# Stick-breaking heads of a Trainium2 kernel: two heads' value products side by side, clamps in two parts, one projection group moved

## What is computed

```python
def stick_breaking_attention(q, k, v):     # 6 heads, 512 tokens, 64 channels
    z = einsum(q, k)                                        # scores
    log_fail = where(valid, log_sigmoid(-z), 0.0)           # valid: key strictly before query
    after = cumsum(log_fail, reverse=True) - log_fail       # over the keys behind
    wts = where(valid, exp(log_sigmoid(z) + after), 0.0)
    return einsum(wts, v)
...
mixed = concatenate([o_dilated, o_differential, o_stick]) ; return mixed @ w_out
```

## Time and profile before

| | us |
|---|---|
| median of 3 runs | 3336.99 (3336.99 to 3346.36) |
| the profiled execution | 3350.7 |
| its span | 3348.8 |
| PE busy in the span | 3169.2 (95%) |
| DVE busy | 1861.8 (56%) |
| ACT busy | 1261.1 (38%) |

### The profile page before, as it was taken

The page is one execution under the profiler, slowest core; times in us unless marked ns, Lnnn a source line. Parts: engine busy times, 40 slices in busy tenths (PEclk is TensorE's granted clock), DMA queues, the critical chain, the costliest instruction groups (busy, mean ns, idle before and its releaser), DMA issues.

```text
span 3348.8 us, 60877 instructions
## 1 busy us (share of the span) xinstructions
PE 3169.2 (95%) x26440; PEld 2493.3 (74%) x26440; DVE 1861.8 (56%) x2741; ACT 1261.1 (38%) x2098; POOL 179.6 (5%) x168
## 2 busy tenths in 40 slices
PE   7999789999998888999999999999999999999999
PEld 6866677875443234999876679988999876679987
DVE  4366656557121114886355358854886355358853
ACT  3227433322000002453345544433443345544432
POOL 0003222221000000000000000000000000000000
PEclk8999799999999999999999999999999999999999
DMA  7140000114999996333321113323233321123322
GB/s 268 51 151 25 3 4 4 57 34 164 396 407 422 421 421 266 101 101 114 113 82 51 51 63 114 114 96 106 89 113 114 114 82 51 51 63 114 105 92 88
DMA packets 179764, 441.64 MB, mean 132 GB/s; under 512 B 7602, under 2 KB 107692, under 8 KB 154924
## 3 DMA queue, kind: packets, MB, share of 16 engines
q1 hardware_dynamic: 179500, 437.74, 35.4%
HBM read 435.62 MB, written 2.10 MB: 131 GB/s over the span
## 4 chain that ended last, share of the span: by engine, by line
PE 74%; DMA 8%; DVE 6%; ACT 3%; issue 2%; POOL 0%; SPq 0%; DVEq 0%; POOLq 0%; ACTq 0%
PE banks L3624 7%; PE banks L3622 7%; PE banks L3625 7%; PE banks L4023 7%; PE banks L2734 5%; PE banks L3744 4%; PE banks L3742 4%; PE banks L3743 4%; DMA ring<-in_exp_w_down 3%; DMA ring<-in_exp_w_gate 3%; DMA ring<-in_exp_w_up 1%; PE banks L350 1%; PE banks L394 1%; PE banks L1818 1%; PE banks L1673 1%
## 5 line engine op out<-in xcount | busy, mean ns | idle before, releaser
L2734 PE MATMUL banks<-ring,arena 128*64 128x512 f32 x1120 | 262.5, 605 | 36.8 <-DMA ring<-in_exp_w_gate 13.8
L3744 PE MATMUL banks<-tail_r,hid_r 128*128 128x512 f32 x704 | 278.3, 395 | 0.0
L3742 PE MATMUL banks<-tail_r,two_r 128*128 128x512 f32 x640 | 254.3, 397 | 0.0
L3743 PE MATMUL banks<-ring_r,two_r 128*128 128x512 f32 x640 | 248.0, 388 | 0.0
L2734 PEld LDWEIGHTS banks<-ring,arena 128*64 128x64 f32 x1120 | 86.1, 139 | 199.8 <-issue 185.4
L3622 PE MATMUL banks<-ring_r,tail_r 128*128 128x256 f32 x624 | 175.7, 282 | 9.1 <-DVE arena L3707 9.1
L305 DVE TENSOR_TENSOR hid_r<-arena,two_r 128x1024 fp32r<-128x1024 f32 x40 | 49.1, 1227 | 235.7 <-ACT two_r L302 221.4
L3624 PE MATMUL banks<-h_r,tail_r 128*128 128x256 f32 x624 | 175.7, 282 | 0.0
L3624 PE MATMUL banks<-ring_r,tail_r 128*128 128x256 f32 x624 | 175.5, 281 | 0.0
L3622 PE MATMUL banks<-mix_r,tail_r 128*128 128x256 f32 x624 | 174.3, 279 | 0.0
L3625 PE MATMUL banks<-ring_r 128*128 128x256 f32 x608 | 171.4, 282 | 0.0
(11 more groups left out here) (611 smaller groups left out, 8627.2 us busy)
## 6 DMA issues: line engine op xcount, KB each, us to landing
ring<-in_exp_w_gate SPq DMA_DIRECT2D x62, 1024.0 KB, 23.0
ring<-in_w_ffn_gate SPq DMA_DIRECT2D x44, 1024.0 KB, 5.4
ring<-in_w_ffn_up SPq DMA_DIRECT2D x44, 1024.0 KB, 5.4
ring<-in_exp_w_down SPq DMA_DIRECT2D x40, 1024.0 KB, 23.2
ring<-in_w_ffn_down SPq DMA_DIRECT2D x20, 2048.0 KB, 7.9
ring<-in_exp_w_up SPq DMA_DIRECT2D x38, 1024.0 KB, 19.0
ring<-in_w_in SPq DMA_DIRECT2D x13, 2048.0 KB, 10.1
arena<-in_exp_w_up SPq DMA_DIRECT2D x26, 1024.0 KB, 23.5
```

The lines of the kernel that those rows point to most:

```text
L2734: ins = TE.matmul(banks[64 * e:64 * e + 64, b0 + hf, :], lhs(kk, e), w[:, k, hf * 512:(hf + 1) * 512], start=(kk == 0), stop=(kk == KD - 1))
L3742: TE.matmul(bank, h_hi, w_hi[:, c, ns], start=(f == 0), stop=False)
L3743: TE.matmul(bank, h_hi, w_lo[:, c, ns], start=False, stop=False)
L3744: ins = TE.matmul(bank, h_lo, w_hi[:, c, ns], start=False, stop=(f == NF - 1))
```

## The change

- The last projection group leaves the 12 chunks (`END = len(gs) - 1`). It is fixed to bank 6 and issued in one piece in `st_pe`, behind after_sums(0). The other three last groups are spread over the 12 chunks, 6 matmuls each. Its copy out follows exp(0) on ACT. `part_of_group` becomes a function of the mixer, otherwise as it was.
- `after_sums` names its first part, bank 0 or 3, `zc0`. The clamp is made in two instructions, of 512 columns (`clamped0`, after `zc0`) and 768 columns (`clamped`, after `zc`). `z(i)` waits for `clamped0` of head i-2 before its first score matmul and for `clamped` before its second.
- `values(p, tiles_)` multiplies heads 2p and 2p+1 together, alternating: for each key tile first the one head, then the other, into the two halves of one bank. For pairs 0 and 1 it is issued in two parts, key tile 0 and key tiles 1 to 3.
- `wt` has four places. `out_copy` copies 128 partitions for two heads, three times in place of six.
- `sub_sums` moves behind after_sums(1), the variance on DVE behind the clamp of head 1, ACT's ln and exp of it from turn 2 to turn 3.
- The next load into the ring's first slot waits for `pv` of the last pair.

PE's new order is: z1, sums0, last group, z2, sums1, sub_sums, z3, sums2, values(0; tile 0), z4, sums3, values(0; tiles 1 to 3), z5, sums4, values(1; tile 0), sums5, values(1; tiles 1 to 3), tile(0, 0), tile(0, 1), values(2; all).

```diff
-                    LAST = len(gs) - NT
+                    LAST, END = len(gs) - NT, len(gs) - 1
-                    total, ending = units_in(gs[OPEN:LAST]), units_in(gs[LAST:])
+                    total, ending = units_in(gs[OPEN:LAST]), units_in(gs[LAST:END])
...
+                    bank_at[len(gs) - 1], bank_free[len(gs) - 1] = 6, last_in[6]
...
-                    wt = region(hT_at + 1536, 2, 1280)
+                    wt_homes = [region(sb_at, 1280), region(body + 3 * T, 1280), region(hT_at + 1536, 1280), region(hT_at + 2816, 1280)]
+                    wt = lambda h: wt_homes[h % 4]
...
-                    slot_user[first % RING] = (nm, "all_turned", N - 1)
+                    slot_user[first % RING] = (nb, "pv", 2)
...
                         if i >= 2:
-                            l.wait_ge(*past(nb, "clamped", i - 2))
+                            l.wait_ge(*past(nb, "clamped0", i - 2))
...
+                            if s_ == 1 and i >= 2:
+                                l.wait_ge(*past(nb, "clamped", i - 2))
...
+                        def values(p, tiles_):
...
+                            for j in tiles_:
                                 oj = where[j][2]
+                                for h in (2 * p, 2 * p + 1):
+                                    po = half(h)
+                                    ins = TE.matmul(banks[po:po + HD, 6 + p % 2, j * P:T], vt[:, j, 640 + h * HD:640 + (h + 1) * HD],
+                                                    wt(h)[:, oj:oj + T - j * P], start=(j == 0), stop=(j == NT - 1))
...
                         z(l, 1)
+                        after_sums(0)
+                        part_of_group(l, len(gs) - 1, 0, len(gs[-1]["mms"]))
+                        z(l, 2)
+                        after_sums(1)
+                        l.wait_ge(*past(nb, "squares"))
+                        l.wait_ge(*past(nm, "read", len(gs) - 1))
+                        for k in range(2):
+                            ins = TE.matmul(banks[:, 6 + k, :], ones2, sq2[:, k, :], start=True, stop=True)
+                        l.did(ins.then_inc(l.sem, 1), nb, "sub_sums")
+                        z(l, 3)
+                        for i in (2, 4):
                             after_sums(i)
+                            values(i // 2 - 1, (0,))
+                            if i == 2:
+                                z(l, 4)
+                            after_sums(i + 1)
+                            values(i // 2 - 1, (1, 2, 3))
+                            if i == 2:
+                                z(l, 5)
...
-                            if i == 2:
+                            if i == 3:
                                 l.wait_ge(*past(nb, "sub_var"))
                                 l.did(S.activation(rs2, sq2, ACT.Ln).then_inc(l.sem, 1))
...
+                                if h == 0:
+                                    group_out(l, len(gs) - 1)
+                                if h in (3, 5):
+                                    l.wait_ge(*past(nb, "pv", h // 2 - 1))
+                                    out_copy(l, h // 2 - 1)
...
+                                for key, c0, c1, ended_ in (("zc0", 0, T, "clamped0"), ("zc", T, 1280, "clamped")):
+                                    l.wait_ge(*past(nb, key, h))
+                                    l.did(V.tensor_scalar(wt(h)[:, c0:c1], flat(h)[:, c0:c1], 0.0, None, ALU.min).then_inc(l.sem, 1), nb, ended_, h)
+                                if h == 1:
+                                    l.wait_ge(*past(nb, "sub_sums"))
```

More of the change, by code:

```diff
@@ L4002, in beside @@
                             split_unit(l, u, k0, k1)
-                    def w_pe(l):
[L4005 to L4027, removed]
@@ new lines, in part_of_group @@
+                    def part_of_group(l, i, j0, j1):
+                        g = gs[i]
+                        if j0 == 0:
+                            if i == 0:
+                                for t in (2, 3):
+                                    l.wait_ge(*past(early, "lo", t))
+                            l.wait_ge(ring_full[g["loads"][0] % RING], g["loads"][1])
+                            l.wait_ge(*past(nm, "lo", g["unit"]))
+                            if i >= OPEN and bank_free[i] is not None:
+                                l.wait_ge(*past(nm, "read", bank_free[i]))
+                            elif i >= OPEN and bank_of(i) == 5:
+                                k_, g_ = [kg for kg in turn_no if turn_bank(*kg) == 5][-1]
+                                l.wait_ge(*past(nm, "T", k_, g_))
+                        for m in g["mms"][j0:j1]:
+                            bank = banks[:, bank_of(i), :]
+                            if i < 2:
+                                ins = TE.matmul(m[1](bank)[:, T // 2:T], m[2], m[3][:, T // 2:T], start=m[4], stop=m[5])
+                            else:
+                                ins = TE.matmul(m[1](bank), m[2], m[3], start=m[4], stop=m[5])
+                        if j1 == len(g["mms"]):
+                            l.did(ins.then_inc(l.sem, 1), nm, "made", i)
+                            l.name_last(nm, "used", g["unit"])
+                            l.name_last("freed", g["loads"][0])
@@ L4305, in after_sums @@
                                                     start=False, stop=(m == later[s_][-1][0]), skip_group_check=True)
+                                if s_ == 0:
+                                    l.did(ins.then_inc(l.sem, 1), nb, "zc0", i)
                             l.did(ins.then_inc(l.sem, 1), nb, "zc", i)
[L4308 to L4315, removed]
-                                oj = where[j][2]
-                                ins = TE.matmul(banks[po:po + HD, 6 + h % 2, j * P:T], vt[:, j, 640 + h * HD:640 + (h + 1) * HD],
-                                                wt[:, h % 2, oj:oj + T - j * P], start=(j == 0), stop=(j == NT - 1))
-                            l.did(ins.then_inc(l.sem, 1), nb, "pv", h)
@@ L4320, in st_pe @@
-                        z(l, 1)
-                        for i in range(6):
-                            after_sums(i)
[L4323 to L4337, removed]
+                        def values(p, tiles_):
+                            if tiles_[0] == 0:
+                                for h in (2 * p, 2 * p + 1):
+                                    l.wait_ge(*past(nb, "exp", h))
+                                if p == 2:
+                                    l.wait_ge(*past(nb, "o", 0))
+                                else:
+                                    l.wait_ge(*past(nb, "sub_var"))
+                            for j in tiles_:
+                                oj = where[j][2]
+                                for h in (2 * p, 2 * p + 1):
+                                    po = half(h)
+                                    ins = TE.matmul(banks[po:po + HD, 6 + p % 2, j * P:T], vt[:, j, 640 + h * HD:640 + (h + 1) * HD],
+                                                    wt(h)[:, oj:oj + T - j * P], start=(j == 0), stop=(j == NT - 1))
+                            if tiles_[-1] == NT - 1:
+                                l.did(ins.then_inc(l.sem, 1), nb, "pv", p)
@@ L4338, in st_pe @@
+                        l.wait_ge(*past(nb, "clamped", 4))
+                        tile(0, 0)
                         l.wait_ge(*past(nb, "clamped", 5))
                         tile(0, 1)
-                        values(5)
+                        values(2, (0, 1, 2, 3))
                     def st_act(l):
```

42 lines of the change are left out of this document (18 added, 24 removed).

## The result

| | us |
|---|---|
| before, median of 10 runs | 3343.81 (3336.99 to 3348.51) |
| changed, median of 10 runs | 3323.97, lowest 3316.94 |
| ratio | 0.9947, 95% interval 0.9933 to 0.996 |
| ratio in a second set, 5 runs of the changed kernel | 0.9938, 0.9925 to 0.9951 |

The change makes the kernel faster by 18 us (13 to 22), in the second set by 21 (16 to 25). The ratios leave out two of the ten executions, 3540.1 us at a mean granted clock of 0.84 (the first that was profiled) and 10305.8 us, and likewise one of 5798.5 us of a later version.

What follows compares the result with a forecast made beforehand. PE, busy 95% of the span, was taken as the bound. Gains of 11.3 us in layer 0 and 9.9 in layer 1, plus z(5)'s earlier 0.1 each, made 21.4: median 3337.0 becomes 3315.6 us, range 3308 to 3326.

Steps and rivals of the forecast that it cites:

- the clock at 1.00 over the whole stage: Stick stage, both layers: granted clock expected to stay 1.00, gaining 4.67 us in layer 0 and 3.31 in layer 1.
- the prediction's own last sign: Profile after the change: a half clock behind z(5), or value blocks near 4.6 us, would make the prediction wrong.
- Values of two heads: Value products in the stick stage: a pair of heads costs 2.30 us like one head, gaining 6.56 us a layer.
- The wait at z(2) and the clock behind it: PE before z(2): 2.71 us idle goes, and half clock behind it, worth 4.67 us in layer 0, 3.31 in layer 1.
- The wait at z(1): PE before z(1): a new wait for the last projection group's end and copy, 0.65 us, between 0 and 1.2.
- The wait at z(5): PE before z(5): a new wait of 2.0 us (0 to 3) behind ACT's ln, exp, splits and DVE's first clamp.
- PE's arrival: PE would reach z(5) 12.4 us after the end of z(3), while z(5)'s inputs took some 14.4.
- The step that failed: Clock behind z(5): the sum charged only the 2.0 us wait there, with the clock staying at 1.00.
- the rival: Clock falls behind the wait before z(5): 3.3 to 4.7 us a layer, 8 together, so 3323.6 us; chance 0.15.
- what was worked out from it: Value pairs, passes starting strictly in order: key tile 0 +0.43 us, 1.2 a layer, so 3318.0 us; chance 0.24.
- Queues, copies, banks: Second `w_out` load some 7 us later, hidden by over 30 us; slot wait and three wider copies cost nothing.

## Where the prediction was right, and where it failed

**The direction and the size.** 21.4 us were forecast; 18 (13 to 22) and 21 (16 to 25) were measured. The forecast of 3315.6 rested on a median of 3337.0 for the kernel before. Over ten runs that kernel has 3343.8, 6.8 more, which is most of the 8.4 by which the changed kernel's median is above the forecast. The median of 3324.0 is in the range of 3308 to 3326, near its upper end. The windows, which do not have this scatter, give 17.4: the forecast's 21.4, less 5.0 for half clock behind z(5), and 1.0 more since z(5) waits 0.5 less in each layer. So the time came out near the forecast although one of its conditions, the clock at 1.00 over the whole stage, was not met. By the prediction's own last sign, a half clock behind z(5), it was wrong there.

**Values of two heads.** Right. Rows of 128 columns told the cost at 512: 1.01, 1.45 and 2.31 where 1.02, 1.45 and 2.30 were said, and 6.57 a layer in place of 6.56.

**The wait at z(2) and the clock behind it.** Right in size, 2.71 + 4.67 and 2.71 + 3.31, which the kernel before with only the variance moved gives as 64.99 - 57.54 = 7.5 and 63.62 - 57.53 = 6.1. The reason was told by halves. The prediction let the moved group cover the clamp. The variance's place alone does it in the kernel before, and in the changed kernel z(2) waits neither with the group nor without it.

**The wait at z(1).** Forecast 0.65, measured 0.67. That the group goes to bank 5 and the copy has to be waited for was read from one start time in the earlier trace rows.

**The wait at z(5).** Forecast 2.0, measured 1.52. The chain from softplus(3) to softplus(4) took 11.20 us where the sum had 11.42, since ACT's instructions overlap by 0.1 each. From the start of softplus(4) to z(5) it took 2.75 (1898.60 to 1901.35) where the sum had some 3.0 with its handovers. PE's arrival was as said: its last pass ended 12.43 us after the start of softplus(3), and the sum had 12.4.

**The step that failed** is the one that held the wait at z(5) to be free of consequences for the clock. In the sum the clock behind this wait stands at nothing; the runs showed half clock behind it in every layer of the changed kernel, 3.3 or 6.7 us long, which costs 5.0 us for both layers. The prediction gave the rival 0.15 and weighed 2.0 us against an idle of 2.09 in the experts that had no such effect. It took idle time alone as the measure, from one case. What stands around a wait matters too: behind z(5)'s wait come eight passes of 64 rows, and where they had 128 the clock held in 4 layers of 4. Which property of the work decides is open, as the waits before L394 and z(1) show. The rival's price was too high, 5 us in all and not 8, because it was taken from 2.71 us of idle, with 10.2 and 6.7 us of half clock behind it. Behind 1.5 us there were 3.3 to 6.8.

Here a page of the Trainium skill bears on the trace. TensorE: Matmul & The Clock Gate, section What's actually happening, says that the clock follows how busy PE has been of late. The rows agree, in that half clock follows idle at z(2) before the change and at z(5) after it. The same page's rule that matmuls start strictly in order (Part 3: Packing small matmuls — row/col tiling) did not cost what was worked out from it. The profile has the two heads' first passes starting together at 1890.83, ahead of the first head's second pass at 1891.31, and 1.01 us, not 1.45. With head after head, the second head's first pass at 1927.94 stands ahead of passes of the first at 1928.15. Here the measurement differs from the page, and it decides.

**Queues, copies, banks.** The later `w_out` load, the slot and the wider copies cost nothing visible: the stretch between the stages is shorter by what the moved group explains, and the one behind the last is as long as it was.

## What to carry to other kernels

An in-order engine pays for what stands in front of an instruction, needed or not: ask of each short wait on PE what its releaser had been waiting for, and whether that can go behind. Two products with 64 output channels, alternated into the two halves of the array, cost here what one did (2.31 us for both, 2.30 for one). A wait on PE of more than a us should be priced with the clock behind it: here 1.7 or 3.3 us for a wait of 1.5. Two splits on ACT, moved behind what PE waits for, took that wait away.

## What the hardware showed unexpectedly

- An idle of 1.5 us on PE in front of fp32 matmuls of 64 rows was followed by 3.3 to 6.8 us at half clock in 8 layers of 8. Idles of 1.70 in front of the same matmuls on 128 rows were not (4 of 4), nor was the one of 2.09 in the earlier trace rows, of 128 rows as well. But 1.54 or 1.55 us in front of L394, also of 128 rows, was in 4 of 12 profiled executions.
- 0.67 us of idle in front of such a z was followed by 3.3 us of half clock in 1 layer of 12.
- The same idle in the same kernel was followed by 3.3 us of half clock in two layers and by 6.7 in two.
- Two heads' rows of passes that follow each other in the program still overlap in part: 2.2 us a layer lost by head after head, where no overlap would be 3.4.
